# Causal attention of a hybrid decoder step: bank pairs by unit parity, scores issued up to two units ahead, both heads in one DVE operation, and 32 small copies moved

## The chip, the cores and the metric

The kernel runs on one core of a Trainium2 chip. The metric is device time in microseconds (us) of the whole program; the shorter the better. Four engines do the work here: TensorE (PE, with its weight loads as PEld), VectorE (DVE), ScalarE (ACT) and GpSimd (POOL); SP issues most of the DMAs. Each engine works through its own list of instructions in order and waits on semaphores.

## What is computed

One inference step of a decoder layer for a prompt of 1024 tokens and 8 sample tokens: a mixer of two branches (an mLSTM and a latent attention), then cross-attention into a memory, then a SwiGLU FFN. The change touches the latent attention of the prompt. Cut to that:

```python
def mla_attention(q_lat, q_rope, ckv, kr, pos0, ckv_past, kr_past):
    # prompt: ckv_past is None; 8 heads, nope 64 + rotary 32, v 64
    def attend_block(args):                      # a block of 128 queries
        ql, qr, start = args
        s = (einsum('bqhr,bkr->bhqk', ql, ckv) + einsum('bqhd,bkd->bhqk', qr, kr)) * scale
        s = where(kpos[None, :] <= qpos[:, None], s, -inf)
        p = softmax(s, axis=-1)
        return einsum('bhqk,bkr->bqhr', p, ckv)
    ...
```

The kernel computes it in the form that is not absorbed: per-head keys and values are made first, then scores, softmax and values per head.

## The kernel before, in words

The program is one long list for each engine, written by hand in the order in which it runs; semaphores named in the code carry every dependency. The stage that matters here lies between 653 and 887 us of the profiled span: ahead of it PE makes per-head queries, keys and values (`att_step`, the last is "v3", evacuated by ACT), behind it comes the decode of the 8 samples against the paged cache (`dec_step`), whose first cache pages are gathered by POOL before, and whose further pages POOL gathers once the last unit is done (it waits for `att_values_done`).

The attention runs in 32 **units** (`UNITS`): a pair p of heads (0 to 3) times a block i of 128 queries (0 to 7). A unit's keys are the (i + 1) x 128 that are not masked as a whole. For p = 0 and 2 the blocks go upward, i = 0 to 7, for p = 1 and 3 downward, i = 7 to 0, so units 0 to 15 are one sweep up and down, and 16 to 31 another. Units with i of 0 to 3 are called **narrow** (at most 512 keys, one PSUM bank per head), those with i of 4 to 7 **wide** (two banks per head). A unit u is worked on like this; `s(u)` below is short for its scores, and so on:

- `att_scores` (PE, L1210 nope part, L1215 rotary part): scores of both heads into PSUM banks 0 to 3, head j in banks 2j and 2j + 1. It waits until the exps of the unit before are done, since those read the same banks.
- `att_max` (DVE, L2324 to L2326): adds the causal mask to the last 128 columns, takes the row maximum, scales it; one after the other for the two heads.
- `att_exp` (ACT, L1796): exp with the maximum as bias and the sum as accumulator, one instruction for each head.
- DVE L2333 and L2335: reciprocal of the sum, and the probabilities are scaled by it, per head.
- `att_turn` (PE, L1234): transposes the probabilities of both heads into banks 4 and 5, four blocks of 128 at a time; ACT copies the first four blocks out (L1804), DVE the further ones of wide units (L2341).
- `att_values` (PE, L1248): values of both heads into bank 6 or 7; DVE copies them out (L2343).

PE's loop over u is: `att_scores(u + 1)`, `att_turn(u)`, `att_values(u)`. This is called **body** u below. ACT's body is the copies of u, then the exps of u + 1; DVE's is the scaling of u, `att_max(u + 1)`, its share of the copies of u, and the copy of the values of u.

Ahead of the stage DVE also copies the rotary queries of the samples into the table `QR` (L2309, 32 copies of 32 x 8) and the latent queries into `QL` (L2313, out of banks 6 and 7), for the decode.

## Time and profile before

| | |
|---|---|
| time, median of 3 runs | 2654.67 us (2653.75 to 2670.62) |
| the profiled execution: its own time | 2670.82 us |
| its span, first to last instruction | 2669.0 us |
| mean granted TensorE clock | 0.935 of full |
| PE busy | 2428.6 us (91%) |
| DVE, ACT busy | 962.7 us (36%), 729.9 us (27%) |
| the attention stage | 653 to 887 us, 234 us |

Busy time is time in which an engine has an instruction under way. In the rows further down, a row of the timeline merges neighbouring instructions of one line: its start, the time from its first start to its last end, the engine, the line, what it does and how many, and in brackets how long the engine stood idle before it and for whom. A granted clock of 1.00 is 2.4 GHz, 0.50 is 1.2 GHz.

### The profile page before, as it was taken

To read this page: it belongs to the slowest core of one execution; us is meant where nothing else is said; L and a number is where in the kernel's file an instruction comes from. 1 tells how busy PE (TensorE), PEld (TensorE's weight loads), DVE (VectorE), ACT (ScalarE), POOL (GpSimd) and SP (SyncE) were. 2 spreads that over 40 slices of the span, in tenths; PEclk is the share of its full clock that TensorE was granted. 3 is DMA by queue.
4 is the path that set the end of the run, shared out by engine and by line. 5 is a ranking of instruction groups with operands and counts; after the bars stand their busy time and mean duration, and the time that the engine had idled before them with its cause. 6 is when DMAs were issued, how large, how long until landed. Compare 5 with 4: busy or idle time off the path is not lost.

```text
span 2669.0 us, 37151 instructions
## 1 busy us (share of the span) xinstructions
PE 2428.6 (91%) x15726; PEld 2039.8 (76%) x15726; DVE 962.7 (36%) x1692; ACT 729.9 (27%) x1128; POOL 321.4 (12%) x382
## 2 busy tenths in 40 slices
PE   5999899999989899888999797985999999989994
PEld 5999899984444676665666466954999999989994
DVE  3452233343465544442101514127111111145556
ACT  5322222222233444442002103023111111134442
POOL 0000011102000577760200000000000000000000
PEclk9999999999688999998999898597999999999997
DMA  4223333332000687862231103011111111111121
GB/s 122 56 80 95 95 104 103 110 104 89 1 1 1 233 234 235 234 199 95 95 103 40 40 8 142 1 48 72 48 45 42 47 47 47 53 44 43 43 85 64
DMA packets 186467, 223.22 MB, mean 84 GB/s; under 512 B 18089, under 2 KB 148598, under 8 KB 185734
## 3 DMA queue, kind: packets, MB, share of 16 engines
q1 hardware_dynamic: 155238, 114.33, 13.9%
q0 software_dynamic: 31136, 107.56, 12.6%
q8 instruction: 69, 1.13, 0.2%
q14 instruction: 24, 0.20, 0.0%
HBM read 191.88 MB, written 29.98 MB: 83 GB/s over the span
## 4 chain that ended last, share of the span: by engine, by line
PE 79%; DVE 7%; POOL 5%; ACT 3%; issue 3%; DMA 2%; SPq 0%; POOLq 0%; ACTq 0%; DVEq 0%
PE ps L1384 18%; PE ps L912 16%; PE ps L1196 13%; PE ps L1575 9%; POOL mem L842 2%; POOL mem L843 2%; PE ps L1210 2%; PE ps L1215 2%; PE ps L1278 1%; PE ps L1082 1%; PE ps L1248 1%; DVE mem L2325 1%; PE ps L1308 1%; PE ps L1532 1%; PE ps L1503 1%
## 5 line engine op out<-in xcount | busy, mean ns | idle before, releaser
L1196 PE MATMUL ps<-mem 128*128 128x344 f32 x1152 | 340.2, 459 | 5.4 <-DMA mem<-w_out 4.2
L1196 PEld LDWEIGHTS ps<-mem 128*128 128x128 f32 x1152 | 222.1, 193 | 122.7 <-issue 11.4
L912 PE MATMUL ps<-stream_first,early_first 128*128 128x344 f32 x912 | 298.2, 327 | 4.3 <-DVE H_short L2038 3.0
L912 PE MATMUL ps<-H_short,early_first 128*128 128x344 f32 x912 | 293.7, 322 | 0.0
L912 PE MATMUL ps<-stream_first,ring_short 128*128 128x344 f32 x912 | 293.4, 322 | 0.0
L1384 PE MATMUL ps<-stream_first,sel_short 128*128 128x344 f32 x1056 | 225.4, 322 | 15.7 <-DVE H_short L2578 15.7
L1384 PE MATMUL ps<-H_short,sel_short 128*128 128x344 f32 x1056 | 224.9, 321 | 0.0
L1384 PE MATMUL ps<-stream_first,ring_short 128*128 128x344 f32 x1056 | 223.7, 320 | 0.0
L1384 PEld LDWEIGHTS ps<-stream_first,sel_short 128*128 128x128 f32 x1056 | 178.3, 189 | 17.4 <-issue 13.4
L912 PEld LDWEIGHTS ps<-stream_first,early_first 128*128 128x128 f32 x912 | 173.9, 191 | 13.1 <-ACT mem L1707 6.1
L1384 PEld LDWEIGHTS ps<-H_short,sel_short 128*128 128x128 f32 x1056 | 179.5, 190 | 0.0
L1384 PEld LDWEIGHTS ps<-stream_first,ring_short 128*128 128x128 f32 x1056 | 176.7, 189 | 0.0
L912 PEld LDWEIGHTS ps<-H_short,early_first 128*128 128x128 f32 x912 | 173.6, 190 | 0.0
L912 PEld LDWEIGHTS ps<-stream_first,ring_short 128*128 128x128 f32 x912 | 173.4, 190 | 0.0
L2610 DVE TENSOR_TENSOR gates_short<-hidden_raw,H_short 128x1032 fp32r<-128x1032 f32 x88 | 108.5, 1234 | 118.9 <-ACT H_short L1960 118.9
L2461 DVE TENSOR_TENSOR ring_short<-ring_raw,sel_short 128x1024 fp32r<-128x1024 f32 x44 | 53.8, 1223 | 236.6 <-ACT sel_short L1855 236.6
L1278 PE MATMUL ps<-mem 128*128 128x128 f32 x1024 | 124.6, 276 | 4.0 <-ACT mem L1810 3.9
L1960 ACT ACTIVATE H_short<-hidden_raw 128x1032 fp32r<-128x1032 f32 x88 | 93.7, 1066 | 124.9 <-PE ps L1575 124.9
L843 POOL DMA_INDIRECT mem<-cache_krope,mem x128 | 121.6, 950 | 39.0 <-issue 38.1
L1575 PE MATMUL ps<-H_short 128*128 128x344 f32 x528 | 113.3, 323 | 13.0 <-DVE gates_short L2610 13.0
L842 POOL DMA_INDIRECT mem<-cache_ckv,mem x128 | 120.8, 944 | 34.8 <-issue 31.5
L1278 PEld LDWEIGHTS ps<-mem 128*128 128x128 f32 x1024 | 114.7, 142 | 7.4 <-ACT mem L1810 7.3
(411 smaller groups left out, 3443.1 us busy)
## 6 DMA issues: line engine op xcount, KB each, us to landing
ring_raw<-w_ffn_in SPq DMA_DIRECT2D x44, 512.0 KB, 3.6
ring_raw<-w_in SPq DMA_DIRECT2D x37, 512.0 KB, 3.9
ring_raw<-w_ffn_out SPq DMA_DIRECT2D x16, 704.0 KB, 4.3
branch_gates<-mem POOLq DMA_DIRECT2D x16, 516.0 KB, 4.5
mem<-branch_gates SPq DMA_DIRECT2D x2, 4128.0 KB, 15.0
chunks_apart<-mem POOLq DMA_DIRECT2D x12, 516.0 KB, 2.9
mem<-chunks_apart POOLq DMA_DIRECT2D x8, 768.0 KB, 5.7
residual_stream<-mem SPq DMA_DIRECT2D x8, 516.0 KB, 2.6
```

What stands on the lines that cost most here:

```text
L842: pool.indirect_dma_start(ukv[s][:, g].rearrange("p r c -> p (r c)"), None, ckv_rows, at).then_inc(kv_in[s], 16)
L843: pool.indirect_dma_start(ukr[s][:, g], None, kr_rows, at).then_inc(kv_in[s], 16)
L912: mm = pe.matmul(ps[:, bank, 0:TN], w[:, k], x[:, k, j * TN:(j + 1) * TN], start=(k == 0 and q == 0), stop=(k == KT - 1 and q == 2))
L1196: mm = pe.matmul(ps[0:m, s + j, 0:TN], w[:, k], x[:, j * TN:(j + 1) * TN], start=(k == 0), stop=(k == kts - 1))
L1210: pe.matmul(ps[:, 2 * j + b, 0:w], q_nope[rows, p, i * P:(i + 1) * P], k_nope[rows, p, b * 512:b * 512 + w], start=True, stop=False)
L1215: mm = pe.matmul(ps[:, 2 * j + b, 0:w], q_rope[rows, p // 2, i * P:(i + 1) * P], k_rope[rows, b * 512:b * 512 + w], start=False, stop=True)
L1278: mm = pe.transpose(ps[:, b + r // 2, (r % 2 * 2 + k) * P:(r % 2 * 2 + k + 1) * P], ukv[s][:, g, r, k * P:(k + 1) * P], ident)
L1384: mm = pe.matmul(ps[:, s + j, 0:TN], w[:, k], x[k][:, j * TN:(j + 1) * TN], start=(k == 0 and q == 0), stop=(k == KT - 1 and q == 2))
L1575: mm = pe.matmul(ps[:, 3 * m + j, 0:TN], w[:, kk], x[:, j * TN:(j + 1) * TN], start=(k == 0 and n == 0), stop=(k == FT - 1 and n == 2))
L1960: act.activation(hid_hi[k % 2], hid_raw[:, k], ACT.Copy).then_inc(tile_hi, 1)
L2461: dve.tensor_tensor(wlo[n % WSLOT], wraw[n % WSLOT], whi[n % 2].bitcast(F32), ALU.subtract).then_inc(weights_rest_ok, 1)
L2610: dve.tensor_tensor(hid_lo[k % 2], hid_raw[:, k], hid_hi[k % 2].bitcast(F32), ALU.subtract).then_inc(tile_lo, 1)
```

## The change

1. `att_bank`: narrow units use one bank for each head, and the pair is chosen by the unit's parity: banks 0 and 1 for even u, 2 and 3 for odd u. Wide units use all four as before.
2. `used_before(u)` is the last unit before u that used one of its banks; `att_scores(u)` now waits for the exps of that unit, not of unit u - 1.
3. `NEXT[u]` lists the units whose scores body u issues: u + 1 if it is not issued yet, and u + 2 if its banks were last used by unit u or an earlier one. In runs of narrow units body u thus issues the scores of u + 2; among wide units it issues u + 1 as before; where narrow units meet wide ones, a body issues two, or none. ACT's exps and DVE's maxima follow the same list.
4. `att_max` handles both heads with one instruction each (mask, maximum, scaling), and one reciprocal serves both heads; so `att_scored` and `att_max_ok` count units, and the first head's exp waits for the maximum of both.
5. The copy of the values of a unit (`att_out`) moves into the next body of DVE, ahead of that body's `att_max`.
6. The 32 copies into `QR` move from ahead of the stage into DVE's bodies 4 to 11 (four each, i = 4 to 7 and 7 to 4), and PE waits for the latent queries after the first `att_turn`, not before the first scores.

```diff
+        def att_bank(u, j, b):
+            return 2 * j + b if UNITS[u][1] >= 4 else 2 * (u % 2) + j
...
+        def used_before(u):
+            return max([v for v in range(u) if att_banks(v) & att_banks(u)], default=-1)
+
+        NEXT, seen = [], 1
+        for u in range(NUA):
+            NEXT.append([v for v in range(seen, NUA) if v <= u + 1 or v == u + 2 and used_before(v) <= u])
+            seen += len(NEXT[u])
...
             def att_scores(u):
-                if u:
-                    pe.wait_ge(att_exp_ok, 2 * u)
+                if used_before(u) >= 0:
+                    pe.wait_ge(att_exp_ok, 2 * used_before(u) + 2)
...
-            pe.wait_ge(att_queries_ok, 1)
             att_scores(0)
             for u in range(NUA):
-                if u + 1 < NUA:
-                    att_scores(u + 1)
+                for v in NEXT[u]:
+                    att_scores(v)
                 att_turn(u)
+                if u == 0:
+                    pe.wait_ge(att_queries_ok, 1)
                 att_values(u)
...
             def att_exp(u):
+                act.wait_ge(att_max_ok, u + 1)
+                if u >= 2:
+                    act.wait_ge(att_turned, TURNS[u - 1])
                 for j in range(2):
-                    act.wait_ge(att_max_ok, 2 * u + j + 1)
...
             def att_max(u):
-                for j in range(2):
-                    dve.wait_ge(att_scored, 2 * u + j + 1)
-                    src = ps[:, 2 * j:2 * j + 2].rearrange("p b c -> p (b c)")
-                    step.step(dve.tensor_tensor(src[:, i * P:(i + 1) * P], src[:, i * P:(i + 1) * P], neg, ALU.add))
-                    step.step(dve.tensor_reduce(mx[:, j:j + 1], src[:, 0:(i + 1) * P], AX.X, ALU.max))
-                    dve.tensor_scalar(nb[:, j, u % 2:u % 2 + 1], mx[:, j:j + 1], -SCALE, None, ALU.mult).then_inc(att_max_ok, 1)
+                dve.wait_ge(att_scored, u + 1)
+                src = att_area(u)
+                o = src[:, :, i * P:w]
+                step.step(dve.tensor_tensor(o, o, neg.rearrange("p (o c) -> p o c", o=1).broadcast_to([P, 2, P]), ALU.add))
+                step.step(dve.tensor_reduce(mx[:, u % 2], src, AX.X, ALU.max))
+                dve.tensor_scalar(nb[:, u % 2], mx[:, u % 2], -SCALE, None, ALU.mult).then_inc(att_max_ok, 1)
...
             att_max(0)
             for u in range(NUA):
+                dve.wait_ge(att_exp_ok, 2 * u + 2)
+                step.step(dve.reciprocal(rl[:, u % 2], lsum[:, u % 2]))
                 for j in range(2):
-                    dve.wait_ge(att_exp_ok, 2 * u + j + 1)
-                    step.step(dve.reciprocal(rl[:, j:j + 1], lsum[:, j, u % 2:u % 2 + 1]))
...
+                if 4 <= u < 12:
+                    h = u - 4
+                    rows = slice(h % 4 * ROPE, (h % 4 + 1) * ROPE)
+                    for r in range(4):
+                        step.mark(dve.tensor_copy(QR[r * ROPE:(r + 1) * ROPE, r, :, h:h + 1], ...
+                if u:
+                    att_out(u - 1)
+                for v in NEXT[u]:
+                    att_max(v)
```

**PE at the start of the stage.** Line, operation, output and input, the output's partitions and columns, and how often (L1210 and L1215 of before are L1230 and L1235 now: scores; L1234 is L1253: transposes; L1248 is L1267: values). Before, scores 0 to 3 and the first units:

```order
L1210 MATMUL ps<-mem 128x128 x2
L1215 MATMUL ps<-mem 128x128 x2
L1210 MATMUL ps<-mem 128x256 x2
L1215 MATMUL ps<-mem 128x256 x2
L1234 MATMUL ps<-mem 128x128 x2
L1248 MATMUL ps<-mem 64x128 x2
L1210 MATMUL ps<-mem 128x384 x2
L1215 MATMUL ps<-mem 128x384 x2
L1234 MATMUL ps<-mem 128x128 x4
L1248 MATMUL ps<-mem 64x128 x4
L1210 MATMUL ps<-mem 128x512 x2
L1215 MATMUL ps<-mem 128x512 x2
```

Now, from the scores of unit 1 on:

```order
L1230 MATMUL ps<-mem 128x256 x2
L1235 MATMUL ps<-mem 128x256 x2
L1230 MATMUL ps<-mem 128x384 x2
L1235 MATMUL ps<-mem 128x384 x2
L1253 MATMUL ps<-mem 128x128 x2
L1267 MATMUL ps<-mem 64x128 x2
L1230 MATMUL ps<-mem 128x512 x2
L1235 MATMUL ps<-mem 128x512 x2
L1253 MATMUL ps<-mem 128x128 x4
L1267 MATMUL ps<-mem 64x128 x4
L1253 MATMUL ps<-mem 128x128 x6
L1267 MATMUL ps<-mem 64x128 x6
```

Three units' scores stand ahead of the first transposes, and the last four rows are bodies 1 and 2 with no scores between them, since the next scores are those of a wide unit. Body 18 looks the same.

**ACT at the turn from unit 14 to 17 (i = 1, 0, 0, 1).** L1796 is now L1818 (exps), L1804 is L1826 (copies of transposed probabilities). Before:

```order
L1796 ACTIVATE mem<-ps,mem 128x256 x2
L1804 ACTIVATE mem<-ps 128x256 x2
L1796 ACTIVATE mem<-ps,mem 128x128 x2
L1804 ACTIVATE mem<-ps 128x128 x2
L1796 ACTIVATE mem<-ps,mem 128x128 x2
```

Now:

```order
L1818 ACTIVATE mem<-ps,mem 128x256 x2
L1826 ACTIVATE mem<-ps 128x384 x2
L1818 ACTIVATE mem<-ps,mem 128x128 x2
L1826 ACTIVATE mem<-ps 128x256 x2
L1818 ACTIVATE mem<-ps,mem 128x128 x2
L1826 ACTIVATE mem<-ps 128x128 x2
```

One unit's copies and the next unit's exps now stand between a unit's exps and its own copies.

**DVE in a wide unit (the second of the stage's wide units, i = 5).** L2333 and L2335 (reciprocal, scaling) are now L2356 and L2358; L2324 to L2326 (mask, maximum, scaling of it) are L2341 to L2343; L2341 (copies) is L2374; L2343 (values out) is L2349; L2365 are the copies into `QR`. Before (i = 4):

```order
L2333 RECIPROCAL mem<-mem 128x1
L2335 TENSOR_SCALAR mem<-mem 128x640
L2333 RECIPROCAL mem<-mem 128x1
L2335 TENSOR_SCALAR mem<-mem 128x640
L2324 TENSOR_TENSOR ps<-ps,mem 128x128
L2325 TENSOR_REDUCE mem<-ps 128x1
L2326 TENSOR_SCALAR mem<-mem 128x1
L2324 TENSOR_TENSOR ps<-ps,mem 128x128
L2325 TENSOR_REDUCE mem<-ps 128x1
L2326 TENSOR_SCALAR mem<-mem 128x1
```

Now (i = 5):

```order
L2356 RECIPROCAL mem<-mem 128x2
L2358 TENSOR_SCALAR mem<-mem 128x768 x2
L2365 COPY mem<-mem 32x8 x4
L2349 COPY mem<-ps 128x128
L2341 TENSOR_TENSOR ps<-ps,mem 128x2x128
L2342 TENSOR_REDUCE mem<-ps 128x2
L2343 TENSOR_SCALAR mem<-mem 128x2
L2374 COPY mem<-ps 128x256 x2
```

Between the scaling and the maxima now stand four copies into `QR` and the values of the unit before; the maxima of both heads are three instructions in place of six.

## Rows read from the trace of the kernel before

**Rows 1.** The page: span and instructions.
```profile
span 2669.0 us, 37151 instructions
```

**Rows 2.** Busy time by engine in four stretches, then granted clock, DMA share, GB/s.
```profile
655.30:709.90 54.60, 49.77 (x198) 25.06 (x198) 23.34 (x71) 15.46 (x40) 0.00 (x0) 0.50 0.00 1
709.90:774.80 64.90, 55.47 (x434) 31.24 (x434) 44.91 (x127) 25.50 (x60) 0.00 (x0) 1.00 0.00 1
774.80:815.70 40.90, 37.22 (x146) 18.27 (x146) 18.47 (x57) 11.64 (x30) 0.00 (x0) 0.50 0.00 1
815.70:887.00 71.30, 60.79 (x471) 34.03 (x470) 46.90 (x130) 27.95 (x62) 0.51 (x2) 1.00 0.00 1
```

**Rows 3.** Waits, 653 to 887 us: who waited for whom, us, times, longest.
```profile
DVE ps L2324 <- PE ps L1215: 71.9, 27, 12.2
PEld ps L1248 <- DVE mem L2341: 11.2, 11, 1.5
```

**Rows 4.** PE's timeline at the start of the stage: scores of units 1 and 2.
```profile
656.27 1.23 PE L1210 MATMUL ps<-mem 64*128 64x256 f32 x4 [2.18 <-ACT mem L1796]
661.13 1.65 PE L1210 MATMUL ps<-mem 64*128 64x384 f32 x4 [0.81 <-ACT mem L1796]
```

**Rows 5.** PE's timeline at the turn: bodies 13 to 19 begin with L1210 rows.
```profile
764.01 0.70 PE L1210 MATMUL ps<-mem 64*128 64x256 f32 x4
...
767.82 0.49 PE L1210 MATMUL ps<-mem 64*128 64x128 f32 x4
...
768.67 0.82 PE L1234 MATMUL ps<-mem 128*128 128x128 f32 x4
...
770.98 0.49 PE L1210 MATMUL ps<-mem 64*128 64x128 f32 x4 [0.27 <-ACT mem L1796]
...
774.00 0.70 PE L1210 MATMUL ps<-mem 64*128 64x256 f32 x4 [0.78 <-ACT mem L1796]
...
778.22 1.65 PE L1210 MATMUL ps<-mem 64*128 64x384 f32 x4 [0.70 <-ACT mem L1796]
...
788.33 1.54 PE L1234 MATMUL ps<-mem 128*128 128x128 f32 x6
...
792.02 2.08 PE L1210 MATMUL ps<-mem 64*128 64x512 f32 x4
```

**Rows 6.** PE's timeline: starts of bodies 5, 6 and 22 (wide).
```profile
696.75 2.08 PE L1210 MATMUL ps<-mem 64*128 64x512 f32 x4
...
709.96 1.13 PE L1210 MATMUL ps<-mem 64*128 64x512 f32 x4
...
813.85 2.05 PE L1210 MATMUL ps<-mem 64*128 64x512 f32 x4
...
823.12 1.13 PE L1210 MATMUL ps<-mem 64*128 64x512 f32 x4
```

**Rows 7.** Two stretches, decode transposes (L1278) alone: PE, PEld busy, clock, DMA, GB/s.
```profile
887.40:890.80 3.40, 3.40 (x19) 3.40 (x17) 0.50 1.00 359
890.80:894.20 3.40, 1.66 (x15) 1.42 (x13) 0.99 0.95 406
```

**Rows 8.** DVE and ACT by form: shapes, count, busy, mean ns, idle before.
```profile
L2324 DVE TENSOR_TENSOR ps<-ps,mem 128x128 f32<-128x128 f32 x64 | 18.9, 295 | 72.0 <-PE ps L1215 71.9
L2325 DVE TENSOR_REDUCE mem<-ps 128x1 f32<-128x1024 f32 x8 | 9.8, 1225 | 0.3
L2325 DVE TENSOR_REDUCE mem<-ps 128x1 f32<-128x128 f32 x8 | 2.3, 292 | 0.3
L1796 ACT ACTIVATE mem<-ps,mem 128x1024 f32<-128x1024 f32 x8 | 8.9, 1114 | 2.2 <-DVE mem L2326 1.8
L1796 ACT ACTIVATE mem<-ps,mem 128x128 f32<-128x128 f32 x8 | 2.9, 366 | 1.7 <-DVE mem L2326 1.6
```

**Rows 9.** The 32 copies into `QR`: ns shortest, median, longest; first and last start.
```profile
L2309 DVE COPY mem<-mem x32: 151/166/420, 628.9 to 635.8; 32x8 f32<-32x8 f32 x32
```

**Rows 10.** PE's timeline: the transposes of the last unit.
```profile
884.64 0.72 PE L1234 MATMUL ps<-mem 128*128 128x128 f32 x2 [0.78 <-DVE mem L2335]
```

More of the change, by code:

```diff
@@ L182, in build @@
         rowno = small(1)
-        mx = small(2)
+        mx = small(4).rearrange("p (n j) -> p n j", j=2)
         nb = small(4).rearrange("p (j n) -> p j n", j=2)
         lsum = small(4).rearrange("p (j n) -> p j n", j=2)
-        rl = small(2)
+        rl = small(4).rearrange("p (n j) -> p n j", j=2)
         H = view(H_at, KT * T, k=KT)
@@ L588, in build, with att_banks, att_area @@
         WIDE = [sum(i >= 4 for _, i in UNITS[:u]) for u in range(NUA + 1)]
+        def att_bank(u, j, b):
+            return 2 * j + b if UNITS[u][1] >= 4 else 2 * (u % 2) + j
+        def att_banks(u):
+            return {att_bank(u, j, b) for j in range(2) for b in range(UNITS[u][1] // 4 + 1)}
+        def att_area(u):
+            w = (UNITS[u][1] + 1) * P
+            if UNITS[u][1] >= 4:
+                return ps[:, 0:4].rearrange("p (j b) c -> p j (b c)", j=2)[:, :, 0:w]
+            return ps[:, 2 * (u % 2):2 * (u % 2) + 2, 0:w]
+        def used_before(u):
[4 more added lines that the diff above has]
+            seen += len(NEXT[u])
         N_CONST, N_GAINS = 8, 10
@@ L1209, in att_scores @@
                         rows = slice(j * NOPE, (j + 1) * NOPE)
-                        pe.matmul(ps[:, 2 * j + b, 0:w], q_nope[rows, p, i * P:(i + 1) * P], k_nope[rows, p, b * 512:b * 512 + w],
+                        pe.matmul(ps[:, att_bank(u, j, b), 0:w], q_nope[rows, p, i * P:(i + 1) * P], k_nope[rows, p, b * 512:b * 512 + w],
                                   start=True, stop=False)
@@ L1214, in att_scores @@
                         rows = slice(e * ROPE, (e + 1) * ROPE)
-                        mm = pe.matmul(ps[:, 2 * j + b, 0:w], q_rope[rows, p // 2, i * P:(i + 1) * P], k_rope[rows, b * 512:b * 512 + w],
+                        mm = pe.matmul(ps[:, att_bank(u, j, b), 0:w], q_rope[rows, p // 2, i * P:(i + 1) * P], k_rope[rows, b * 512:b * 512 + w],
                                        start=False, stop=True)
-                        if b == i // 4:
-                            mm.then_inc(att_scored, 1)
+                mm.then_inc(att_scored, 1)
             def att_turn(u):
@@ L1793, in att_exp @@
                 w = (i + 1) * P
+                act.wait_ge(att_max_ok, u + 1)
+                if u >= 2:
+                    act.wait_ge(att_turned, TURNS[u - 1])
                 for j in range(2):
-                    act.wait_ge(att_max_ok, 2 * u + j + 1)
-                    act.activation(Pb[j][u % 2][:, 0:w], ps[:, 2 * j:2 * j + 2].rearrange("p b c -> p (b c)")[:, 0:w], ACT.Exp,
-                                   bias=nb[:, j, u % 2:u % 2 + 1], scale=SCALE, accum_out=lsum[:, j, u % 2:u % 2 + 1]).then_inc(att_exp_ok, 1)
+                    act.activation(Pb[j][u % 2][:, 0:w], att_area(u)[:, j], ACT.Exp,
+                                   bias=nb[:, u % 2, j:j + 1], scale=SCALE, accum_out=lsum[:, u % 2, j:j + 1]).then_inc(att_exp_ok, 1)
             att_exp(0)
@@ L2304, in _ @@
             step.join()
-            dve.wait_ge(constants_set, 5)
-            for h in range(AH):
-                rows = slice(h % 4 * ROPE, (h % 4 + 1) * ROPE)
-                for r in range(4):
-                    step.mark(dve.tensor_copy(QR[r * ROPE:(r + 1) * ROPE, r, :, h:h + 1],
-                                              q_rope[rows, h // 4, SEQ:T].rearrange("p (b o) -> p b o", o=1)))
             dve.wait_ge(att_latent_done, 1)
@@ L2320, in att_max @@
                 i = UNITS[u][1]
[L2321 to L2326 removed]
+                w = (i + 1) * P
@@ new lines, in att_max, with att_out @@
+                dve.wait_ge(att_scored, u + 1)
[4 more added lines that the diff above has]
+                dve.tensor_scalar(nb[:, u % 2], mx[:, u % 2], -SCALE, None, ALU.mult).then_inc(att_max_ok, 1)
+            def att_out(u):
+                p, i = UNITS[u]
+                dve.wait_ge(att_values_done, u + 1)
+                dve.tensor_copy(obT[:, p, i * P:(i + 1) * P], ps[:, 6 + u % 2, 0:P]).then_inc(att_out_ok, 1)
@@ L2336, in _ @@
-                if u + 1 < NUA:
-                    att_max(u + 1)
+                    dve.tensor_scalar(Pb[j][u % 2][:, 0:w], Pb[j][u % 2][:, 0:w], rl[:, u % 2, j:j + 1], None, ALU.mult).then_inc(att_probs_ok, 1)
+                if u == 4:
+                    dve.wait_ge(constants_set, 5)
+                if 4 <= u < 12:
+                    h = u - 4
+                    rows = slice(h % 4 * ROPE, (h % 4 + 1) * ROPE)
+                    for r in range(4):
+                        step.mark(dve.tensor_copy(QR[r * ROPE:(r + 1) * ROPE, r, :, h:h + 1],
+                                                  q_rope[rows, h // 4, SEQ:T].rearrange("p (b o) -> p b o", o=1)))
@@ L2338, in _ @@
+                if u:
+                    att_out(u - 1)
+                for v in NEXT[u]:
+                    att_max(v)
                 if i >= 4:
```

11 lines of the change are left out of this document (4 added, 7 removed).

## The prediction

> **What bounds the kernel now.** The span is 2669.0 us [rows 1]. The change touches only the attention stage, 653 to 887 us, so I read that stage alone: first the busy time by stretch, then who waits for whom, then PE's timeline body by body. The stretches [rows 2] show two things. PE is the bound: it is busy 203 of 232 us, DVE 134, ACT 81. And in two stretches, 54.6 and 40.9 us long, its granted clock is 0.50, which is 1.2 GHz; elsewhere it is 1.00. Each slow stretch begins where an upward sweep begins with its smallest units, and both are 91% busy, so there the clock is what costs. In the full-clock stretches PE idles 9.4 and 10.5 us.
>
> What stood before each fall: at the first, PE waited 2.18 us for the exps of unit 0 [rows 4]; at the second it had waited 0.27 and 0.78 us for exps ahead of two neighbouring score blocks [rows 5]. There is nothing else late in the stage: DMA share is 0.00 [rows 2], so the decode's first pages lie ready, and decode and POOL both start from the last unit. What the stage saves reaches the end whole.
>
> **The change part by part.**
>
> *Start.* Scores of unit 1 now use banks 2 and 3 and need no wait. They run in the idle 2.18 us ahead of 656.27 at full clock; today they stand behind it at half clock, 1.23 us for the first half [rows 4], about 2.3 for both. The 0.81 us wait before 661.13 goes. New is a wait: ACT does the exps of unit 1 behind the copies of unit 0, and the scores of unit 3 wait for them. Two exps of 256 columns are about 0.95 us (0.366 at 128, 1.114 at 1024, on a line [rows 8]); the values of unit 0 cover part, and I take 0.35. Gain 2.3 + 0.8 - 0.35 = 2.8 us, with the clock still falling: PE still waits for ACT's last evacuation before the first scores, for the exps of unit 0 before the third, and at each copy.
>
> *The turn (bodies 14 to 18).* The waits 0.27, 0.78 and 0.70 for exps [rows 5] go: scores are issued two units ahead, so the exps they wait for are one body old. What remains is the wait between transposes and values for ACT's copies, which the change doesn't touch. If that keeps the clock up, bodies 16 to 18, today 792.02 - 774.00 = 18.02 us, shorten. Full-clock prices: scores of 128 columns are 768.67 - 767.82 = 0.85 us, each further 128 costs 2 x (0.70 - 0.49) = 0.42; a body less its scores and its exp wait is 3.81 - 1.27 = 2.54 for i = 2, 3.16 - 0.27 - 0.85 = 2.04 for i = 1, 3.02 - 0.78 - 0.85 = 1.39 for i = 0 [rows 5]. So 16 to 18 take (1.27 + 1.39) + (1.69 + 2.04) + (2.11 + 2.54) = 11.0 us.
>
> But body 18 now has no scores, since unit 20 is wide and needs unit 19's banks. Its transposes wait for DVE, which first does the maxima of unit 19. Mask 0.43, maximum 1.23 (1024 columns for two heads [rows 8]), scaling, reciprocal and one probability scaling: about 2.6 us behind the scores, of which unit 17's transposes and values cover 2.04. That leaves 0.55 idle, then another wait for copies with ACT still in unit 19's exps. I take it that the clock falls there: the transposes and values of unit 18 then cost 792.02 - 788.33 = 3.69 us [rows 5], not 2.54. Gain 18.0 - 11.0 - 0.55 - 1.15 + 0.27 + 0.78 = 6.3 us. From below: the clock falls where it does today, and only the waits (1.75), scores of unit 17 at full clock (0.4) less 0.1 at body 18 are left, 2.0. From above, bodies 19 to 21 at full clock too; worked out with the rivals, 14.8.
>
> I weigh one rule here. From 887.4 to 890.8 us, at the start of the decode, PE does nothing but transposes at clock 0.50, and the stretch behind it stands at 0.99 [rows 7]: transposes brought the clock back. The Trainium skill ("TensorE: Matmul & The Clock Gate", Part 4: PE-mode transpose) says that transposes do not count as PE activity in the same way and the full clock doesn't engage for them. By the rule the turn, much of which is transposes, would lose its clock as before, and the sum would have 2.0 in place of 6.3; the row speaks against it, so I keep it as a rival.
>
> *Wide units.* One maximum for both heads saves two fixed parts and a scaling: about 0.4 us a unit (a reduction of 128 costs 0.292, of 1024 1.225, so the fixed part is 0.16 [rows 8]). That brings DVE's copies forward, for which PE waits 11.2 us in 11 places [rows 3]. Against it: the first head's exp now waits for both maxima, so the last exp ends later by the exp's own time less 0.47, that is 0.64 us at 1024 columns and 0.32 at 640, and the next scores wait for it. Walking the twelve full-clock wide bodies (6 to 11, 21 to 26) with both chains, bodies with two large units gain (0.28, 0.41, 0.16 each sweep), the others lose (0.2, 0.1; 0.5, 0.2, 0.1): gain 0.6 us. From both sides: gain 4.4 if the copies alone decide (11 x 0.4), loss 5.8 if the exps alone do (three bodies each of 0.32, 0.43, 0.54, 0.64). I take 0.6, as the walk has both in nearly equal parts.
>
> *The 32 copies.* A median of 0.166 us [rows 9], with their issue about 0.9 us a unit. Removing them ahead of the stage gains nothing: DVE waits 12.2 us for the first scores. In units 4 to 11 the wait of DVE for scores hides them (71.9 us in 27 places, 2.7 each [rows 3]); uncovered they would cost 8 x 0.9 = 7 us. Behind them stand the copy of the values (nobody needs it for a whole body) and the maxima.
>
> *End.* The 0.78 us before the last transposes [rows 10] goes, as unit 31's exps are a body earlier.
>
> Sum: 2.8 + 6.3 + 0.6 + 0.8 = 10.5 us. The profiled execution took 2670.8 us, so 2660.3 on its level. The median of the runs shown is 16.2 us below that execution, one of three runs at its level; I can't see from one trace where those 16 us lie. I take the same cut from the median: 2654.7 - 10.5 = 2644.2 us.
>
> **Rivals.**
>
> 1. *The turn loses the clock as today.* 2.8 + 2.0 + 0.6 + 0.8 = 6.2: 2648.5 us. For it: the copies' waits stay. Against: units 12 to 14 go through such waits today at full clock.
>
> 2. *The clock holds through an upward sweep.* Bodies 19 to 21 take 823.12 - 792.02 = 31.1 us today [rows 5, 6]. At full clock their scores are 2.96, 3.38 and 3.80, and behind them the chain mask, two maxima, two exps and hand-overs (0.82 + twice maximum and exp of one head) is 4.06, 4.54 and 5.02 us: 23.8 in all. That adds 7.3 + 1.15: 2635.7 us. If the first sweep holds too, bodies 0 to 5 go from 53.7 us (656.27 to 709.96 [rows 4, 6]) to 11.0 + 23.8, 16 us more than the 2.8 of the start: 2619.7 us. Against both: the chain leaves PE idle 1 us and more in bodies 19 to 21.
>
> 3. *Slower: the merged maximum costs the clock in wide units.* After the clock has come back, bodies 21 and 22 wait for DVE's copies and then for the later exps, 1.1 us in all. Today such a wait is up to 1.5 us [rows 3] and the clock stands; it decides if the two together do what the one does not. A wide body at half clock costs 13.21 (body 5) against 9.27 (body 21) [rows 6], 3.9 us; five of them 19.7: 2664 us for one sweep, 2684 for both.
>
> **How the numbers follow.** Forecast 0.45, rival 1 0.2, rival 2 0.25 (one sweep 0.15, both 0.1), rival 3 0.1 (both sweeps 0.04). The range reaches from rival 2's both sweeps, 2619, to the forecast on the slower level and rival 3's one sweep, 2665. A measurement can tell about 1% from no change. Below 2628 us: rival 2 in both sweeps, and in one with the clock back a body earlier elsewhere, 0.2. Above 2681: rival 3 in both sweeps, and a little for the copies uncovered, 0.05. Else 0.75.
>
> **What would show it.** Right: scores of units 0 and 1 back to back; no exp wait before score blocks of narrow units; the second slow stretch begins at unit 18 or 19 and the first where it does today; the stage is some 10 us shorter and the decode is as long as before. Wrong: the second fall lies at unit 15 or 16 again (rival 1); no half clock in a sweep (rival 2); half clock in units 22 to 26, or long waits before wide score blocks for exps (rival 3); a decode that grows by what the stage lost.

## The result and the profile after

The changed kernel took 2642.47 us (median of 6 executions, 2637.55 to 2649.78), the kernel before 2664.26 us (6 executions, 2653.75 to 2670.62). The ratio is 0.9932 with a 95% interval of 0.9905 to 0.9959: 18 us less, between 11 and 25. The forecast said 10.5 us less. Its time, 2644.2 us, was met all the same, since it counted from 2654.67 us, and the kernel before lay higher in most later executions (medians of 2656 to 2665 us in the comparisons below). So the time came out and the size did not; where the gain is larger than the sum is what the runs below look for.

The profiled execution after took 2649.78 us (span 2646.7) against 2670.82 before (span 2669.0 [rows 1]); both lie at the slow end of their kernel's six executions. I answer the stretches of [rows 2] first: busy time by engine (PE, PEld, DVE, ACT, POOL), then granted clock, DMA share, GB/s.

```profile
658.20:699.20 41.00, 37.28 (x146) 18.50 (x146) 17.84 (x49) 12.33 (x34) 0.00 (x0) 0.50 0.00 1
699.20:864.60 165.40, 141.64 (x1090) 78.56 (x1086) 103.91 (x236) 66.20 (x158) 0.00 (x0) 1.00 0.00 1
```

In this execution there is one half-clock stretch where there were two: the first sweep still falls at its start, the second doesn't fall at all. PE's timeline of the changed kernel, at the places of [rows 4 to 6] and [rows 10] (start, us, what, and in brackets the idle time before it and for whom; L1230 scores, L1253 transposes, L1267 values, L1287 the decode):

```profile
656.10 0.49 PE L1230 MATMUL ps<-mem 64*128 64x128 f32 x4 [1.11 <-ACT mem L1763]
...
656.94 0.70 PE L1230 MATMUL ps<-mem 64*128 64x256 f32 x4
...
659.12 1.65 PE L1230 MATMUL ps<-mem 64*128 64x384 f32 x4 [0.84 <-ACT mem L1818]
...
706.52 1.13 PE L1230 MATMUL ps<-mem 64*128 64x512 f32 x4 [0.81 <-ACT mem L1818]
...
749.68 1.13 PE L1230 MATMUL ps<-mem 64*128 64x512 f32 x4 [0.29 <-ACT mem L1818]
...
777.29 0.87 PE L1253 MATMUL ps<-mem 128*128 128x128 f32 x6 [0.65 <-DVE mem L2358]
779.11 0.88 PE L1267 MATMUL ps<-mem 128*64 128x128 f32 x12 [0.94 <-ACT mem L1826]
779.91 1.13 PE L1230 MATMUL ps<-mem 64*128 64x512 f32 x4
...
786.90 1.13 PE L1230 MATMUL ps<-mem 64*128 64x512 f32 x4 [1.01 <-ACT mem L1818]
...
794.79 1.13 PE L1230 MATMUL ps<-mem 64*128 64x512 f32 x4 [1.08 <-ACT mem L1818]
...
803.58 1.13 PE L1230 MATMUL ps<-mem 64*128 64x512 f32 x4 [0.81 <-ACT mem L1818]
...
846.74 1.13 PE L1230 MATMUL ps<-mem 64*128 64x512 f32 x4 [0.29 <-ACT mem L1818]
...
864.16 0.44 PE L1267 MATMUL ps<-mem 128*64 128x128 f32 x4 [0.52 <-ACT mem L1826]
864.98 0.65 PE L1287 MATMUL ps<-mem 128*128 128x128 f32 x4 [0.39 <-DVE mem L2349]
```

The scores of units 0 and 1 stand back to back, body 18 (777.29 and 779.11) waits first for DVE and then for copies, and the later wide bodies wait 0.5 to 1.1 us for exps. Of the narrow units' scores only those of units 2, 12 and 28 still wait for exps (0.84, 0.29 and 0.29 us). From such rows comes the table with which all runs are compared: the stage cut into five pieces at the starts of the scores of units 0, 7, 12, 23 and 28 and of the first decode transposes (656.10, 706.52, 749.68, 803.58, 846.74, 864.98 here).

| us | before | after | less |
|---|---|---|---|
| start: scores 0 to scores 7 | 56.78 | 50.42 | 6.4 |
| wide: 7 to 12 | 43.95 | 43.16 | 0.8 |
| turn: 12 to 23 | 69.21 | 53.90 | 15.3 |
| wide: 23 to 28 | 43.95 | 43.16 | 0.8 |
| end: 28 to the decode | 19.58 | 18.24 | 1.3 |
| stage | 233.47 | 208.88 | 24.6 |

The spans differ by 22.3 us and not by 24.6, since the scores of unit 0 began at 653.18 before and at 656.10 after. The half clock ahead of 600 us summed to 30.7 us in the one execution and 37.5 in the other; in a second profile of the changed kernel (below) unit 0 began at 652.98 with 30.7 again. So that difference belongs to the execution. The decode and all behind it took 1782.4 us before and 1781.7 after.

The waits, as in [rows 3] (who waited for whom, us in total, times, longest), first the one of score blocks for exps before, then three after:

```profile
PEld ps L1210 <- ACT mem L1796: 9.5, 16, 2.4
```

```profile
DVE ps L2341 <- PE ps L1235: 60.5, 28, 12.2
PEld ps L1230 <- ACT mem L1818: 11.2, 19, 1.3
PEld ps L1267 <- DVE mem L2374: 7.1, 10, 1.1
```

The wait for DVE's copies fell from 11.2 to 7.1 us. The waits of score blocks for exps went from 9.5 to 11.2 us in all, but they have moved: where PE itself idled for them (6 places before, 9 after), it was always ahead of narrow blocks before, and after it is mostly ahead of wide ones (4.8 of 6.2 us).

### The profile page after: what moved, and what is told of

The parts are those of the page before. It is cut to its first block, busy times and chain, and to the rows that moved or that the text cites. A ratio compares the mean times of both kernels' runs of the same rounds, so it can differ in the third digit from the quotient of the medians.

```text
span 2646.7 us, 37053 instructions
## 1 busy us (share of the span) xinstructions
PE 2406.8 (91%) x15726; PEld 2029.4 (77%) x15726; DVE 944.5 (36%) x1564; ACT 728.3 (28%) x1128; POOL 321.6 (12%) x382
## 3 DMA queue, kind: packets, MB, share of 16 engines
q8 instruction: 68, 1.11, 0.2%
## 4 chain that ended last, share of the span: by engine, by line
PE 79%; DVE 7%; POOL 5%; ACT 4%; issue 3%; DMA 2%; SPq 0%; POOLq 0%; ACTq 0%; DVEq 0%
PE ps L1404 19%; PE ps L932 16%; PE ps L1216 13%; PE ps L1595 9%; POOL mem L862 3%; POOL mem L863 2%; PE ps L1230 2%; PE ps L1235 2%; PE ps L1298 1%; PE ps L1102 1%; DVE mem L2342 1%; PE ps L1552 1%; ACT mem L1818 1%; PE ps L1328 1%; PE ps L1523 1%
```

## The experiments

Pieces in us as above; half clock is the total length at 0.50 within the stage; times are medians. Pieces and half clock come from one profiled execution of each kernel, which can lie well off its median. "Fillers" are matmuls (or, in one kernel, transposes) that write into a PSUM bank whose content nobody reads, at places where PE would stand idle.

| kernel | time | half clock | start | wide | turn | wide | end |
|---|---|---|---|---|---|---|---|
| before (profile) | 2664.26 | 95.6 | 56.78 | 43.95 | 69.21 | 43.95 | 19.58 |
| after (profile) | 2642.47 | 41.0 | 50.42 | 43.16 | 53.90 | 43.16 | 18.24 |
| dve_alone | 2668.46 | 34.2 | 46.29 | 43.17 | 61.70 | 43.16 | 19.55 |
| banks_alone | 2648.60 | 20.5 | 42.03 | 44.04 | 54.90 | 44.03 | 18.47 |
| one_ahead | 2654.78 | 27.3 | 41.65 | 43.16 | 60.29 | 43.16 | 19.16 |
| start_early | 2643.10 | 20.5 | 43.20 | 43.16 | 55.50 | 43.16 | 18.24 |
| before_fill | 2648.32 | 54.6 | 56.78 | 43.95 | 56.80 | 43.95 | 19.58 |
| start_fill | 2634.55 | 0 | 37.91 | 43.15 | 53.90 | 43.16 | 18.24 |
| all_fill | 2630.11 | 0 | 37.91 | 43.15 | 53.89 | 43.16 | 18.24 |
| all_fill_heads | 2634.03 | 0 | 37.83 | 43.83 | 53.82 | 43.47 | 18.24 |
| before_all_fill | 2641.52 | 0 | 39.35 | 43.95 | 56.94 | 43.95 | 19.58 |
| all_fill_turns | 2633.74 | 0 | 37.75 | 43.16 | 53.89 | 43.15 | 18.25 |
| after_again | 2647.71 | 51.2 | 52.49 | 43.17 | 55.52 | 43.18 | 18.25 |
| all_fill_again | 2631.63 | 0 | 37.93 | 43.18 | 53.93 | 43.18 | 18.25 |

### The parts apart: dve_alone and banks_alone

dve_alone keeps the merged DVE operations and the moved copies, but goes back to one area for each head and to scores one ahead:

```diff
-            return 2 * j + b if UNITS[u][1] >= 4 else 2 * (u % 2) + j
+            return 2 * j + b
...
-            NEXT.append([v for v in range(seen, NUA) if v <= u + 1 or v == u + 2 and used_before(v) <= u])
+            NEXT.append([v for v in range(seen, NUA) if v <= u + 1])
...
-                if used_before(u) >= 0:
-                    pe.wait_ge(att_exp_ok, 2 * used_before(u) + 2)
+                if u:
+                    pe.wait_ge(att_exp_ok, 2 * u)
```

> The change without bank pairs and without scores two ahead (scores wait for the unit before, banks as before); the merged DVE operations, the later copy of the values and the moved QR copies stay. My theory (the time came from the exp waits ahead of narrow scores and from the clock that then stays up): within 3 us of before, the clock falls at the start and again at units 15 to 17, the second slow stretch some 41 us long. Rival (the merged DVE operations gave the time): 15 to 20 us faster than before.

Measured: ratio to before 1.0019 (0.9987 to 1.0051). Its wide pieces are 0.8 us shorter each, as in the change, which is less than this comparison can tell. Its profiled execution, 2655.01 us, has two half-clock stretches, shorter than before's; the second, expected at some 41 us, is 13.7 us long:

```profile
659.60:680.10 20.50, 17.80 (x66) 7.87 (x64) 8.27 (x23) 5.91 (x18) 0.00 (x0) 0.50 0.00 1
765.50:779.20 13.70, 11.27 (x40) 4.76 (x42) 5.80 (x18) 3.86 (x15) 0.00 (x0) 0.50 0.01 1
```

That profile is faster than this kernel's median by 13 us: one profile doesn't stand for the clock of all executions.

banks_alone has the bank pairs and the scores two ahead; DVE works per head again, and the copies into `QR` stand ahead of the stage:

```diff
-                step.step(dve.tensor_reduce(mx[:, u % 2], src, AX.X, ALU.max))
-                dve.tensor_scalar(nb[:, u % 2], mx[:, u % 2], -SCALE, None, ALU.mult).then_inc(att_max_ok, 1)
+                for j in range(2):
...
+                    step.step(dve.tensor_reduce(mx[:, u % 2, j:j + 1], src[:, j], AX.X, ALU.max))
+                    dve.tensor_scalar(nb[:, u % 2, j:j + 1], mx[:, u % 2, j:j + 1], -SCALE, None, ALU.mult).then_inc(att_max_ok, 1)
```

> The change without the merged DVE operations (maximum, scaling and reciprocal per head, as before) and with the 32 QR copies at their old place; bank pairs and scores two ahead stay. My theory: 15 to 22 us faster than before, as the change, no half clock around units 15 to 20. Rival (narrow units need the merging, because DVE's per-head chain is 0.4 us longer a unit and then PE waits for the probabilities): the second slow stretch comes back, and the time is 0 to 8 us below before.

Measured: 0.9956 (0.9927 to 0.9986), 12 us less (4 to 19), where 15 to 22 were expected. The order of the scores carries most of the gain; wide pieces are as before (44.04 us), so the merged operations are what takes 0.8 to 0.9 us from them. The second fall is there, and short:

```profile
658.90:676.00 17.10, 15.05 (x56) 6.35 (x52) 9.41 (x34) 5.73 (x18) 0.00 (x0) 0.50 0.00 1
...
771.50:774.90 3.40, 3.40 (x16) 1.63 (x16) 0.38 (x2) 0.00 (x0) 0.00 (x0) 0.50 0.00 0
```

### How far ahead: one_ahead

The change with scores one unit ahead (bank pairs stay, as the one line of `NEXT` above shows; the other two edits of dve_alone aren't made).

> The change with bank pairs, but scores one unit ahead only. My theory: scores no longer wait for exps, but the transposes of a narrow unit wait for its probabilities instead, 0.5 to 0.9 us a unit at full clock in bodies 14 to 18, and the clock falls at the turn in most executions: 6 to 15 us slower than the change. Rival (the bank pairs alone are enough): within 2 us of the change.

Measured: 0.9973 (0.9950 to 0.9995), 7 us of the 18. The clock falls in both sweeps of its profile:

```profile
660.20:670.40 10.20, 9.14 (x32) 4.13 (x34) 5.12 (x16) 3.51 (x12) 0.00 (x0) 0.50 0.01 2
...
762.60:779.70 17.10, 15.78 (x56) 7.12 (x58) 7.41 (x20) 5.43 (x16) 0.00 (x0) 0.50 0.00 1
```

PE's idle times at this turn are only the waits for ACT's copies ahead of values; the expected wait of the transposes for their probabilities isn't there:

```profile
757.47 0.66 PE L1267 MATMUL ps<-mem 128*64 128x128 f32 x8 [0.62 <-ACT mem L1826]
...
759.93 0.44 PE L1267 MATMUL ps<-mem 128*64 128x128 f32 x4 [0.46 <-ACT mem L1826]
...
762.68 0.69 PE L1267 MATMUL ps<-mem 128*64 128x128 f32 x4 [0.46 <-ACT mem L1826]
```

No score block waits for an exp here, and yet the clock falls at 762.6, where a body is smallest. So bank pairs alone remove those waits, and removing them is not enough. The change has such waits for copies there too (0.52 us each in bodies 15 and 16), but scores of larger units stand in these smallest bodies. That this is what holds the clock fits the comparison and isn't shown further.

### The clock or the waits at the turn: before_fill

The kernel before, with fillers in bodies 13 to 17. No wait is taken away.

```diff
+                if u in (14, 15, 16):
+                    fill(1, 128 if u == 14 else 256)
                 if u + 1 < NUA:
                     att_scores(u + 1)
                 att_turn(u)
+                if 13 <= u <= 17:
+                    fill(1, 256)
                 att_values(u)
```

> The kernel before with matmuls of 128 to 256 columns, whose results nobody reads, on PE in the idle time of units 13 to 17 (ahead of the scores that wait for exps, and behind the transposes where PE waits for ACT's copies); no other work moves. If the clock is the larger part of the gain at the turn: no half clock from unit 15 on, stage 12 to 17 us shorter, total 12 to 17 us below before. If the removed waits themselves are the gain: 0 to 3 us above before. If the clock falls a little later, at units 18 to 20: 4 to 8 us below.

Measured: 0.9960 (0.9936 to 0.9984); mean 2650.2 us, before's 2660.1 on the same chip: 10 us less, a little under the expected 12 to 17. The profiled stage itself is 12.4 us shorter. The second stretch is gone, the first is as long as before:

```profile
658.50:713.10 54.60, 49.85 (x200) 25.09 (x200) 23.26 (x71) 15.38 (x40) 0.00 (x0) 0.50 0.00 1
713.10:876.90 163.80, 140.18 (x1060) 77.75 (x1058) 109.60 (x308) 64.94 (x152) 0.00 (x0) 1.00 0.00 1
```

And the waits for exps still stand, longer than in [rows 5], at full clock:

```profile
781.39 0.92 PE L1210 MATMUL ps<-mem 64*128 64x384 f32 x4 [1.16 <-ACT mem L1804]
...
786.01 1.13 PE L1210 MATMUL ps<-mem 64*128 64x512 f32 x4 [0.99 <-ACT mem L1804]
```

The turn went from 69.21 to 56.80 us with more work in it and no wait removed. The change's turn is 53.90: of its 15.3 us, 12.4 are the clock's (or more, as the fillers can only lengthen the bodies) and at most 2.9 what the order itself saves.

### The start: start_early and start_fill

start_early lets the scores of unit 0 wait for the evacuation ahead of the last one ("v2" for "v3"); the wait for "v3" moves behind them.

```diff
-            pe.wait_ge(att_evac, ATT_EVAC["v3"])
+            pe.wait_ge(att_evac, ATT_EVAC["v2"])
...
             att_scores(0)
+            pe.wait_ge(att_evac, ATT_EVAC["v3"])
```

> The change, and the first scores wait for the evacuation of v2 (whose banks they take) and not of v3; the wait for v3 stands ahead of the scores of unit 1. My theory: PE's 1.11 us of waiting ahead of the first scores is split, the stage starts about 0.9 us sooner; if the clock still falls at the start, 1 us below the change; if the shorter wait keeps the clock up, 15 to 20 us below the change, with no half clock in the stage.

Measured: 0.9948 (0.9920 to 0.9975), median 2643.1: as the change. The 1.11 us ahead of the scores of unit 0 are gone, and the clock falls all the same:

```profile
655.34 0.49 PE L1230 MATMUL ps<-mem 64*128 64x128 f32 x4
...
656.52 0.70 PE L1230 MATMUL ps<-mem 64*128 64x256 f32 x4 [0.27 <-ACT mem L1764]
...
658.65 1.65 PE L1230 MATMUL ps<-mem 64*128 64x384 f32 x4 [0.79 <-ACT mem L1819]
```

Behind the start this kernel is the change unaltered, and here the clock does fall in body 18, where the forecast had it, for 3.4 us; the turn takes 55.50 us, 1.6 more than in the first profile after:

```profile
771.30:774.70 3.40, 3.40 (x18) 1.56 (x17) 0.34 (x2) 0.00 (x0) 0.00 (x0) 0.50 0.00 0
```

start_fill adds fillers to it: 256 columns ahead of the scores in bodies 1, 4, 5 and 6 and of the transposes in body 2, and 256 to 384 between transposes and values in bodies 0 to 3.

```diff
             att_scores(0)
+            fill(5, 128)
             pe.wait_ge(att_evac, ATT_EVAC["v3"])
...
+                if u in AHEAD:
+                    fill(own, AHEAD[u])
                 for v in NEXT[u]:
                     att_scores(v)
+                    if v == 1:
+                        fill(5, 384)
...
+                if u in FILLED:
+                    fill(own, BEHIND[UNITS[u][1]])
                 att_values(u)
```

> The change with the early first scores (wait for v2, not v3), and matmuls of 128 to 384 columns whose results nobody reads in PE's idle places of bodies 0 to 6. If the clock falls at the start because PE idles there, no half clock in the first sweep: against the change's 17 to 41 us at half clock in that sweep, 8 to 18 us less, 2625 to 2635 us. If the clock falls all the same (the fillers come too late after the idle ahead of the third scores): the same as the change with early scores, or 1 to 3 us slower, since the fillers then run at half clock and delay what is behind them.

Measured: 0.9901 (0.9867 to 0.9935), median 2634.55. The whole stage stands at full clock:

```profile
652.00:852.50 200.50, 175.07 (x1285) 95.51 (x1284) 123.36 (x292) 81.50 (x195) 1.52 (x3) 1.00 0.01 4
```

### Both sweeps: all_fill and all_fill_heads

all_fill has the same fillers in bodies 12 to 22 too:

```diff
-            AHEAD = {1: 256, 4: 256, 5: 256, 6: 256}
-            MIDDLE = {2: 256}
+            AHEAD = {1: 256, 4: 256, 5: 256, 6: 256, 20: 256, 21: 256, 22: 256}
+            MIDDLE = {2: 256, 18: 256}
...
-            FILLED = (0, 1, 2, 3)
+            FILLED = (0, 1, 2, 3) + tuple(range(12, 20))
```

> As start_fill, with such matmuls in bodies 12 to 22 too. If the change's second sweep is already free of half clock in most executions, 0 to 3 us below start_fill, with a smaller spread from run to run; if the fillers are in the way, 1 to 4 us above it.

Measured: 0.9884 (0.9834 to 0.9934), median 2630.11; the profiled stage reads like start_fill's (first piece 37.91, turn 53.89). The means of the two, 2630.4 and 2634.5 us, differ by 4.0 us, which the intervals leave open. A fall in body 18 as in start_early costs 1.6 us; start_fill may have it in some executions, but its profile has none.

all_fill_heads goes back to one maximum for each head in units 4 to 7 and 20 to 23, where PE waits for exps:

```diff
+                if not (u in (4, 5, 6, 7, 20, 21, 22, 23)):
...
+                for j in range(2):
...
+                    step.step(dve.tensor_reduce(mx[:, u % 2, j:j + 1], src[:, j], AX.X, ALU.max))
```

> As all_fill, with the maxima per head again for units 4 to 7 and 20 to 23 alone (upward wide units, where the next scores wait for the last exp). By the chain worked out from the kernel before, the exp of the second head ends 0.3 to 0.6 us sooner in each of these eight: 2 to 3 us below all_fill at full clock. If DVE's copies, which come 0.4 us later, decide instead: 0 to 2 us above.

Measured: 0.9893 (0.9846 to 0.9941), median 2634.03. The gain that I looked for isn't there: the wide pieces are 43.83 and 43.47 us where all_fill has 43.15 and 43.16. But it isn't the split maxima that lengthen them. The bodies that issue split maxima (3 to 6 and 19 to 22) are 0.37 us shorter in each sweep, far less than the 2 to 3 us expected of both. Longer, by 0.84 and 0.47 us, are bodies 7 to 10 and 23 to 26, whose maxima are merged in both kernels. There the scaling of the maximum starts later behind the same maximum (DVE in body 8, the maximum and its scaling, first in all_fill, then here):

```profile
717.84 2.02 DVE L2363 TENSOR_REDUCE mem<-ps 128x2 f32<-128x1792 f32 x1
719.89 0.17 DVE L2364 TENSOR_SCALAR mem<-mem 128x2 f32<-128x2 f32 x1
```

```profile
717.96 2.02 DVE L2364 TENSOR_REDUCE mem<-ps 128x2 f32<-128x1792 f32 x1
720.46 0.17 DVE L2365 TENSOR_SCALAR mem<-mem 128x2 f32<-128x2 f32 x1 [0.48 <-DVE mem L2364]
```

The other such bodies are about 0.1 us longer each, with a smaller delay in the same place. What delays the scaling isn't shown. The difference in time itself (3 to 4 us) is within what the two intervals leave open.

### What is left at full clock: before_all_fill

The kernel before, with fillers over the start and both sweeps.

```diff
+            fill(5, 512)
             pe.wait_ge(att_evac, ATT_EVAC["v3"])
...
+                for w in AHEAD.get(u, ()):
+                    fill(own, w)
                 if u + 1 < NUA:
                     att_scores(u + 1)
                 att_turn(u)
+                if u in FILLED:
+                    fill(own, BEHIND[UNITS[u][1]])
                 att_values(u)
```

> The kernel before with filler matmuls (into a PSUM bank whose content nobody reads) over the start of the stage and the narrow units of both sweeps: one bank pair, scores one ahead, per-head DVE operations, copies at their old place. Nothing is left out. Theory (clock and waits are separate terms): the granted clock never falls in the stage, as with the fillers in the change, and what stays between this kernel and the change with all its fillers (2630.1 us) is the idle time of TensorE that bank pairs and looking ahead remove at full clock, 5 to 8 us: 2635 to 2639. Rival A (the gain is the clock alone): within 2 us of the change with all fillers, 2628 to 2632. Rival B (looking ahead is worth much more than its idle rows even at full clock): 2645 or above with no half clock in the stage. If the clock still falls in the stage, none of them is told apart.

Measured: 0.9905 (0.9880 to 0.9930), median 2641.52; all_fill_again, on the same chip, 2631.63. PE's first rows and the stage's clock:

```profile
657.70 0.49 PE L1210 MATMUL ps<-mem 64*128 64x128 f32 x4 [0.25 <-ACT mem L1760]
...
660.80 0.70 PE L1210 MATMUL ps<-mem 64*128 64x256 f32 x4 [0.27 <-ACT mem L1813]
```

```profile
652.00:861.10 209.10, 186.12 (x1311) 99.79 (x1309) 133.92 (x383) 84.03 (x195) 1.40 (x2) 1.00 0.02 5
```

The old order with a steady clock takes as long as the change without one. By the pieces of the two kernels at full clock the new order is worth 1.4 (start) + 0.8 + 3.0 (turn) + 0.8 + 1.3 (end) = 7.3 us, within the expected 5 to 8. The median lies 2.5 us above the 2635 to 2639 that was expected with it, and 9.9 above all_fill_again's. 2.5 us of that can be the start: unit 0 begins at 655.17 in the one profile and at 657.70 in the other. That isn't the change's doing: the filled change lets unit 0 wait for "v2", and the filled old kernel issues 512 columns ahead of it and waits for "v3". Rival A, the clock alone (2 us at most), falls, and so does rival B (2645 and above).

The pieces hide a loss. In the upward wide bodies 3, 4 and 5 the filled change takes 6.99, 7.89 and 8.79 us, the filled old kernel 6.63, 7.43 and 8.35, and bodies 19 to 21 give the same: 1.26 us more in each sweep, where score blocks wait for the later exps. banks_alone, with a maximum for each head, has 7.44 and 8.36 us in bodies 20 and 21, and the change 7.89 and 8.79. At full clock the merged operations thus cost these bodies more than the 0.8 us that they take from a wide piece; splitting the maxima alone, as in all_fill_heads, gave 0.37 us of it back.

### Transposes as fillers: all_fill_turns

```diff
-                pe.matmul(ps[:, bank, 0:w], ident, k_nope[:, 0, 0:w], start=True, stop=True)
+                for q in range({128: 2, 256: 3, 384: 5}[w]):
+                    pe.transpose(ps[:, bank, q % 4 * P:(q % 4 + 1) * P], k_nope[:, 0, q % 4 * P:(q % 4 + 1) * P], ident)
```

> The change with fillers at the same places and of about the same length, but made of transposes of 128 columns through TensorE (2, 3 or 5 for 128, 256 or 384 columns) in place of matmuls. Nothing is left out. If transposes do not hold the clock (the rule of the Trainium skill, TensorE: Matmul & The Clock Gate, Part 4), half clock returns at the start of the stage, 17 to 55 us of it, as in the change without fillers: 2637 to 2650 us. If they count as any other work of TensorE, which the decode stage of the kernel before suggests (granted clock 0.50 and then 0.99 in a stretch of transposes), no half clock in the stage and the time of the change with matmul fillers, 2627 to 2635.

Measured: 0.9882 (0.9832 to 0.9931), median 2633.74. The stretch of the stage, and the start with its fillers in L1242 between the kernel's own transposes (L1258) and values (L1272):

```profile
652.00:855.00 203.00, 181.90 (x1369) 103.61 (x1368) 124.76 (x295) 83.21 (x199) 3.49 (x5) 1.00 0.03 9
```

```profile
660.25 0.44 PE L1258 MATMUL ps<-mem 128*128 128x128 f32 x2
660.53 0.49 PE L1242 MATMUL ps<-mem 128*128 128x128 f32 x3
661.12 0.44 PE L1272 MATMUL ps<-mem 128*64 128x128 f32 x4
```

With transposes in the gaps the clock stands at 1.00 through both sweeps, and the stage takes as long as with matmuls (196.2 us against 196.5 in all_fill_again). The Trainium skill ("TensorE: Matmul & The Clock Gate", Part 4: PE-mode transpose) says that the full clock doesn't engage for transposes, as they don't count as PE activity in the same way. This run doesn't agree, and [rows 7] didn't either. Both are fp32 transposes: here they stand among matmuls, and in [rows 7] PE did nothing else for the 3.4 us ahead of clock 0.99.

### The change and its fillers once more: after_again and all_fill_again

> The change once more, beside the three others on one chip: 2640 to 2648 us if the first comparison was typical, with half clock once, at the start of the stage. If its half clock lasts 17 instead of 41 us, the length is not a property of the program.

> The change with all fillers of matmuls once more, on one chip with the change, with the kernel before and its fillers, and with the transposes: 2628 to 2633 us, no half clock in the stage, about 12 us under the change. If it lies within 4 us of the change, the gain of the fillers was one of chips or executions.

Measured: the change 0.9928 (0.9892 to 0.9963), median 2647.71, 7 executions from 2631.61 to 2652.20; with all fillers 0.9877 (0.9827 to 0.9926), median 2631.63, 2628.70 to 2633.77. The profile of after_again took 2650.19 us:

```profile
655.10:702.90 47.80, 44.07 (x166) 21.36 (x164) 20.09 (x51) 13.36 (x36) 0.00 (x0) 0.50 0.00 1
702.90:777.90 75.00, 64.33 (x501) 36.01 (x500) 52.32 (x134) 32.55 (x83) 0.00 (x0) 1.00 0.00 1
777.90:781.30 3.40, 3.22 (x16) 1.68 (x16) 0.69 (x2) 0.04 (x1) 0.00 (x0) 0.52 0.00 0
781.30:865.00 83.70, 71.47 (x554) 39.96 (x552) 48.78 (x100) 32.81 (x74) 0.00 (x0) 1.00 0.00 1
```

```profile
776.27 0.88 PE L1253 MATMUL ps<-mem 128*128 128x128 f32 x6 [0.65 <-DVE mem L2358]
778.08 1.55 PE L1267 MATMUL ps<-mem 128*64 128x128 f32 x12 [0.94 <-ACT mem L1826]
```

This is the same program in the same order, with the same two waits in body 18 (0.65 and 0.94 us) as the first profile after. There the twelve values behind them took 0.88 us, here 1.55, and the clock is back 3.4 us later, as in start_early. That costs the turn 1.6 us (55.52 for 53.90). The first stretch is 47.8 us long here, 41.0 in the other profile, 17.1 in start_early, whose scores differ in one wait. Its length isn't set by the program's order. The fastest execution, 2631.61 us, had a mean clock of 0.953, that of the filled kernels on this chip (0.951 to 0.954), and the profiled one 0.943; that it lost no clock at the start is likely, but no trace of it exists.

In both comparisons with the change, its means are 19 to 20 us under before's. Filled, its mean is some 13 us lower still, the fastest version here.

## Why the prediction was right and wrong, step by step

- **The turn (6.3 us, measured 15.3): the step that failed.** The forecast held that the clock falls at body 18 and stays down through bodies 19 to 21, about 30 us. The waits came as worked out, 0.65 us for DVE (0.55 said) and then one for copies. But in the first profile the clock stood, and in after_again and start_early it fell in body 18 for 3.4 us, at a cost of 1.6 us. So the place was right in two of the three profiles of this order, and the length in none. What then happened is rival 2 in one sweep, whose sign was no half clock in a sweep: in the first profile bodies 19 to 21 took 803.58 - 779.91 = 23.7 us, where that rival worked out 23.8 at full clock; and 6.3 + 7.3 + 1.15 = 14.8 for the turn against 15.3.
- **Why rival 2 had too small a chance.** The prediction's one argument against it was that wide bodies leave PE idle 1 us and more. They do: single waits of 0.81 to 1.08 us in bodies 19 to 22, at clock 1.00. In the rows of before, wide bodies at half clock stay there, which says nothing of wide bodies that begin at full clock. before_fill shows those: the same bodies, in their old order and with longer waits ahead of them, run at full clock once the turn has held it.
- **Clock against waits.** At the turn at least 12.4 of the 15.3 us are the clock's (before_fill). In the whole stage the old order loses 56.78 - 39.35 = 17.4 us to 54.6 us of half clock at the start and 69.21 - 56.94 = 12.3 to 40.9 at the turn; the change 12.5 to 41.0 and 14.6 to 47.8 (against 37.91). That is 0.30 to 0.32 us for each us of half clock in these narrow and mixed bodies.
- **The start (2.8, measured 6.4 in that pair of profiles).** Scores 0 and 1 are back to back, and the clock falls where it did, as forecast. Of the 6.4 us, 4.1 are a shorter slow stretch (13.6 us less, at 0.30), which the program doesn't set. What remains is 2.3; after_again gives 4.3 - 6.8 x 0.30 = 2.3 as well. The expected wait of 0.35 us ahead of the scores of unit 3 didn't appear.
- **Wide units (0.6, measured 1.6 in the wide pieces, less 0.4 in body 21).** The walk had the mechanism and the sign of each body: bodies 7 to 9 became shorter, 6 and 10 longer. It summed the bodies from 6 to 10 and from 22 to 26 to 0.55 us a sweep, and they gave 0.79. Body 21, for which it had a loss of 0.5 us, lost 0.44 (8.79 for 8.35 in before_fill, both at full clock), which the table has in the turn. dve_alone ties the gain to the merged operations, as wide pieces of 43.17 us come without any change of banks. Rival 3 is not seen: no half-clock stretch of the change begins in a wide body. Its waits came, 1.0 to 1.1 us for exps ahead of wide score blocks, and the clock stood. In the bodies that were at half clock before (3 to 5, 19 and 20) the sum has no term for the later exps.
- **The copies (0).** They take 0.167 us each (median) in the bodies and cost nothing that the wide pieces show: these are 43.16 us in the sweep whose DVE bodies have them and in the one whose bodies haven't. And PE waits 1.11 us for ACT ahead of the scores of unit 0 before and after: the copies had not been what it waited for.
- **The end (0.8, measured 1.3).** The wait of [rows 10] is gone.
- **The level.** The cut of 16.2 us from the profiled execution to the median was a guess, and the time was met by luck: with 2664.26 us for before, the same sum would have said 2653.8 and missed by 11.
- **Rival 1** didn't come: no profile of the change has half clock at units 15 to 17. It is what one_ahead shows (762.6, between the scores of units 17 and 18), a turn of 60.29 us.

What stays open: in the profiles of start_fill and both all_fill the work behind the stage, which no edit touches, took 1775 to 1776 us, with all_fill_heads and all_fill_turns 1779 and 1780, with the others 1780 to 1784. The earlier end of the stage alone doesn't do that, as all_fill_turns reaches the decode at 851.46, ahead of the three (851.65 to 852.49). The half clock behind the stage sums to 203.5 to 203.9 us in these three and to 208 to 218 in all others; what sets it isn't shown. So of the 13 us that fillers give, only what the pieces show (12.5 at the start for the first profile after, 14.6 and 1.6 for after_again) is tied to the clock of the stage. What in PE's work makes the clock fall, the idle times or the small blocks between them, is not separated either.

## What to carry to other kernels

A short stretch of small bodies can cost more through the clock behind it than through its own waits: price the clock of what follows (here 0.3 us for each us of half clock), and test it with matmuls in the gaps whose results nobody reads, which needs no new order. Look ahead where bodies are smallest, so that large units' scores stand between the small ones; taking the waits alone away may not be enough. Merging two heads' work can cost as much as it saves: here, at full clock, the same edit shortened wide bodies 7 to 9 and lengthened 3 to 6. And take more than one execution of before as the level: a profile's clock is one draw.

## What the runs showed of the hardware

- The same program draws slow stretches of different lengths: 41.0 and 47.8 us at the start for the change, in a stage of 209 and 213 us, and its executions go from 2631.61 to 2652.20 us with mean clocks from 0.953 to 0.943. The kernel before goes from 2650.26 us (0.945) to 2674.81 (0.934) on one chip.
- In before_fill PE idles 1.16 us ahead of a narrow block (781.39) and the clock stays at 1.00, with fillers in the bodies around; in the change it stays there through 1.08 us ahead of a wide block (794.79). Idle times of only 0.46 to 0.62 us stand ahead of a fall where bodies are smallest (one_ahead, 757 to 763).
- In the six profiles with fillers over the start, the clock stays at 1.00 through the whole stage, whether the fillers are matmuls of 128 to 512 columns or transposes. Behind the start, the fillers of all_fill and all_fill_again made no piece longer than in the change by more than 0.03 us (a turn of 53.93 for 53.90).
